# DeltaNet on one core: VectorE makes each slot's low weight tile behind the next slot's steps

## The chip, the core and the metric

The kernel runs on one core of one Trainium2 chip. The metric is the time of one execution on the device in microseconds (us). Engines are named TensorE (PE in the profile, its weight loads PEld), VectorE (DVE), ScalarE (ACT), GpSimd (POOL) and SyncE (SP, which issues most DMAs).

## What is computed

A trunk of two layers over 256 tokens with 2048 channels, all in float32. Layer 0 is a gated DeltaNet with 32 value heads and a feed-forward network; layer 1 is a sparse attention with another feed-forward network. The change touches only the DeltaNet of layer 0:

```python
proj = x @ w_in                                # q, k, v, z, two gates
qkv = silu(causal_depthwise_conv(qkv, conv_w)) # 4 taps
q, k = l2_normalize(q), l2_normalize(k)
o = chunk_gated_delta_rule(q, k, v, g, beta)   # a triangular solve per head and chunk, then a state
o = rms_norm(o, out_norm_g) * silu(z)
return o @ w_out
```

## The kernel before

**Products in three parts.** To keep float32 accuracy at the speed of fp32r, each weight piece is split: ScalarE copies the raw piece (128 x 1024) to W_HI, rounded (`split_hi`, line 1194), and VectorE subtracts, W_LO = raw - W_HI (`split_lo`, line 1627). TensorE then runs 12 matmuls per piece, W_HI with X_HI, W_LO with X_HI, W_HI with X_LO (`products`, lines 733 to 735). Both splits have four buffers (WS = 4), and so has the raw ring (RAWS = 4).

**The counts that tie them.** ScalarE makes the W_HI tile of piece h + 4 once TensorE is done with piece h (`w_used`); VectorE follows once it is there (`hi_ready`); TensorE starts a piece once its low tile is there (`lo_ready`, line 727); SyncE loads the next raw piece into a buffer when its low tile is done (`feed`, line 2210).

**Iterations and slots.** The DeltaNet runs in ten iterations, one for each of eight groups of four heads and two more to drain. Iterations 2 to 6 are one loop and have the same order; 0, 1, 7, 8 and 9 are written out. An iteration has 32 slots. A slot has at most one weight piece (parts qk, v, z of the input projection, out or old of the output projection), and behind it the steps of the delta rule that tables assign to it: SOLVE_STEPS for the group before, PREP_STEPS for the present one. Every engine walks the same 32 slots and does its own part of each step. In the loop, slots 0 to 7 hold qk, 8 to 15 v, and 16 to 31 z and out in pairs. Iterations 1, 7 and 8 have fewer pieces in the upper slots (PIECES_1, PIECES_7, PIECES_8).

**VectorE in a slot.** In `gdn_vector`: first the addition of an output stripe to H (`add_to_h`, line 1652, odd slots of out), then the steps (lines 1858 and 1859), then the low tile of the piece four further on. If the slot is in LO_HELD, this tile is kept back and made behind the next slot's steps (lines 1860 to 1862). Iterations 0 and 9 hold nothing. HI_HELD is the same for ScalarE and is empty.

**Steps that the text names, with VectorE's lines in the loop.** t0 to t3 (line 1802) and u0 to u5 (1808, 1810) in slots 1, 2, 4, 5, 7, 11, 15 and 16: rounds of the triangular inverse; nw (1815, 1816) in 16; ks (1822, 1825) in 21; kkqk (1769, 1774) in 25; osum (1834, 1835) in 26; oscale (1839, 1841) in 27, whose second part waits for GpSimd; init and masks (1780 to 1791) in 29; o_t (1661, tile A_LO or B_LO) in 31; dif (1757) in 7; the convolution taps (1686) in slots 2, 3, 5, 9, 11 and 12. In iterations 1, 7 and 8 the slots differ a little; ks is in 23, 21 and 15, and t2 of iteration 8 in 4.

Of the kernel before, what the change touches and what calls it, by code (L numbers as in the profile page):

```python
# [311 lines left out]


HI_HELD = ()
LO_HELD = (1, 2, 4, 6, 14)


def gdn_steps(it, hs):
# [206 lines left out]
def build(nc, stream, consts, params, tails, w2, gfin, x, xt, out):  # L525
# [18 lines left out]
    with ctx:  # L544
# [1077 lines left out]
        def split_lo(dve, c, h):  # L1622

            if isinstance(c, int) and c + h >= O_END:
                return
            dve.wait_ge(hi_ready, c + (h + 1))
            nc.vector.tensor_tensor(W_LO[:, h % WS, :], raw_piece(h), W_HI[:, h % WS, :].bitcast(f32),  # L1627
                                    SUB).then_inc(lo_ready, 1)
# [216 lines left out]
        def gdn_vector(dve, link, it):  # L1845
# [3 lines left out]
            for hs in range(32):  # L1849
# [10 lines left out]
                if held is not None:  # L1860
                    split_lo(dve, c, held)
                held = h + WS if part and hs in LO_HELD and not first and not last else None
                if part and held is None:
# [635 lines left out]
```

## Time and profile before

| | |
|---|---|
| time, median of 3 | 2801.64 us (2800.51 to 2804.14) |
| the profiled execution | 2803.94 us, span 2802.1 us |
| TensorE matmul busy | 2739.6 us, 98% |
| TensorE weight load busy | 2282.1 us, 81% |
| VectorE busy | 2219.6 us, 79% |
| ScalarE busy | 1648.4 us, 59% |
| mean granted TensorE clock | 0.995 |
| DMA | 493.23 MB, mean 176 GB/s |

The span is the time from the first to the last instruction of the profiled execution. TensorE's busy time is modelled for pipelined matmuls, so gaps between them say more than their sum. The DeltaNet takes the first third of the span, until about 955 us; one looped iteration takes 111.18 us.

### The profile page before, as it was taken

Reading aid. Unit: us, or ns where it says so; the run is one execution under the profiler, and the core shown is the slowest. Engines: PE = TensorE matmul, PEld = TensorE weight load, DVE = VectorE, ACT = ScalarE, POOL = GpSimd, SP = SyncE. Lnnn points to the kernel's source line nnn. Section 1 sums busy time; section 2 is a strip of 40 time slices with the busy share of each in tenths; the row PEclk is TensorE's granted clock in tenths of the full one; section 3 lists DMA queues with packets and bytes.
Section 4 is the critical chain, followed back from the end, with each engine's and each line's share of the span. In section 5 each row is a group of like instructions: output and inputs, shape, how many; then the busy total and the mean of one; then the engine's idle time right before and its main releaser. Section 6 shows DMA issues by size and latency. Waiting matters only on the chain.

```text
span 2802.1 us, 40252 instructions
## 1 busy us (share of the span) xinstructions
PE 2739.6 (98%) x13456; PEld 2282.1 (81%) x13456; DVE 2219.6 (79%) x2727; ACT 1648.4 (59%) x2184; POOL 31.0 (1%) x30
## 2 busy tenths in 40 slices
PE   8999999999988999999999999999999999999998
PEld 6878888888877888888888888888887888888887
DVE  5867877878767788888888876557677888888887
ACT  6766767667665555555555555554555555555554
POOL 0000000000000000000000000000000000000000
PEclk9999999999999999999999999999999999999999
DMA  6534444445433566656666656643345666656664
GB/s 239 181 124 153 159 144 163 156 149 167 158 105 113 166 210 199 198 185 203 198 198 203 198 172 224 222 135 114 106 158 188 207 199 200 199 184 200 198 201 166
DMA packets 135097, 493.23 MB, mean 176 GB/s; under 512 B 15009, under 2 KB 15329, under 8 KB 134625
## 3 DMA queue, kind: packets, MB, share of 16 engines
q1 hardware_dynamic: 133776, 487.82, 52.8%
q10 hardware_dynamic: 1232, 4.23, 0.4%
q8 instruction: 57, 0.93, 0.1%
q14 instruction: 32, 0.25, 0.0%
HBM read 489.86 MB, written 2.13 MB: 176 GB/s over the span
## 4 chain that ended last, share of the span: by engine, by line
PE 65%; issue 29%; DVE 3%; ACT 2%; DMA 1%; POOL 0%; POOLq 0%; DVEq 0%; SPq 0%; ACTq 0%
PE ACC L733 10%; PE ACC L735 10%; PE ACC L734 10%; PE SIDE L943 7%; PE SIDE L944 7%; PE SIDE L945 7%; PE ACC L943 3%; PE ACC L944 3%; PE ACC L945 3%; PE SIDE L741 2%; DVE W_LO L1627 1%; DMA RAW<-stream 1%; PE SIDE L1138 1%; ACT W_HI L1194 0%; ACT WORK L1587 0%
## 5 line engine op out<-in xcount | busy, mean ns | idle before, releaser
L1627 DVE TENSOR_TENSOR W_LO<-RAW,W_HI 128x1024 fp32r<-128x1024 f32 x424 | 511.6, 1222 | 268.9 <-ACT W_HI L1194 265.8
L1194 ACT ACTIVATE W_HI<-RAW 128x1024 fp32r<-128x1024 f32 x424 | 443.3, 1057 | 217.5 <-PE ACC L735 183.8
L1436 ACT ACTIVATE W_HI<-WORK 128x1024 fp32r<-128x1024 f32 x320 | 325.4, 1031 | 345.8 <-PE SIDE L945 232.7
L733 PE MATMUL ACC<-W_HI,X_HI 128*128 128x512 f32 x1216 | 491.2, 404 | 17.7 <-DVE W_LO L1627 17.6
L735 PE MATMUL ACC<-W_HI,X_LO 128*128 128x512 f32 x1216 | 477.6, 393 | 0.0
L734 PE MATMUL ACC<-W_LO,X_HI 128*128 128x512 f32 x1216 | 476.7, 392 | 0.0
L1878 DVE TENSOR_TENSOR W_LO<-WORK,W_HI 128x1024 fp32r<-128x1024 f32 x300 | 364.5, 1221 | 119.0 <-ACT W_HI L1436 116.3
L1436 ACT ACTIVATE W_HI<-RAW 128x1024 fp32r<-128x1024 f32 x328 | 314.8, 980 | 237.0 <-PE ACC L735 141.6
L733 PE MATMUL ACC<-W_HI,A_HI 128*128 128x512 f32 x928 | 370.3, 399 | 0.7 <-issue 0.7
L735 PE MATMUL ACC<-W_HI,A_LO 128*128 128x512 f32 x928 | 362.7, 391 | 0.0
L734 PE MATMUL ACC<-W_LO,A_HI 128*128 128x512 f32 x928 | 362.2, 390 | 0.0
L1878 DVE TENSOR_TENSOR W_LO<-RAW,W_HI 128x1024 fp32r<-128x1024 f32 x268 | 325.3, 1220 | 22.1 <-ACT W_HI L1436 17.3
L943 PE MATMUL SIDE<-W_HI,X_HI 128*128 128x512 f32 x800 | 311.4, 389 | 0.0
L945 PE MATMUL SIDE<-W_HI,X_LO 128*128 128x512 f32 x800 | 311.3, 389 | 0.0
L944 PE MATMUL SIDE<-W_LO,X_HI 128*128 128x512 f32 x800 | 311.3, 389 | 0.0
L733 PEld LDWEIGHTS ACC<-W_HI,X_HI 128*128 128x128 f32 x1216 | 230.0, 189 | 64.2 <-issue 15.6
L735 PEld LDWEIGHTS ACC<-W_HI,X_LO 128*128 128x128 f32 x1216 | 229.8, 189 | 50.4
L734 PEld LDWEIGHTS ACC<-W_LO,X_HI 128*128 128x128 f32 x1216 | 230.6, 190 | 43.6 <-issue 0.2
L735 PEld LDWEIGHTS ACC<-W_HI,A_LO 128*128 128x128 f32 x928 | 174.7, 188 | 37.2
L733 PEld LDWEIGHTS ACC<-W_HI,A_HI 128*128 128x128 f32 x928 | 174.9, 188 | 36.9 <-issue 2.3
L734 PEld LDWEIGHTS ACC<-W_LO,A_HI 128*128 128x128 f32 x928 | 174.9, 188 | 36.0 <-issue 1.2
L1652 DVE TENSOR_TENSOR H<-H,ACC 128x1024 f32<-128x1024 f32 x135 | 164.3, 1217 | 14.9 <-PE ACC L735 14.6
(363 smaller groups left out, 3798.7 us busy)
## 6 DMA issues: line engine op xcount, KB each, us to landing
RAW<-stream SPq DMA_DIRECT2D x752, 512.0 KB, 4.6
WORK<-stream SPq DMA_DIRECT2D x160, 512.0 KB, 4.8
WORK<-gdn_rows ACTq DMA_DIRECT2D x8, 512.0 KB, 6.2
WORK<-xt SPq DMA_DIRECT2D x4, 512.0 KB, 9.3
H<-x SPq DMA_DIRECT2D x2, 1024.0 KB, 13.6
out<-WORK SPq DMA_DIRECT2D x4, 512.0 KB, 3.5
WORK<-tails SPq DMA_DIRECT2D x2, 512.0 KB, 10.8
WORK<-gfin SPq DMA_DIRECT2D x1, 1024.0 KB, 6.6
```

The source lines that it names most:

```text
L733: nc.tensor.matmul(dst, hi[:, at:at + P], wh, start=first and h % 2 == 0 and q == 0, stop=False)
L734: nc.tensor.matmul(dst, hi[:, at:at + P], wl, start=False, stop=False)
L735: m = nc.tensor.matmul(dst, lo[:, at:at + P], wh, start=False, stop=last and h % 2 == 1 and q == 1)
L741: m = nc.tensor.transpose(SIDE[p][:, to:to + P], src, ident)
L943: nc.tensor.matmul(dst, hi, wh, start=start, stop=False)
L944: nc.tensor.matmul(dst, hi, wl, start=False, stop=False)
L945: return nc.tensor.matmul(dst, lo, wh, start=False, stop=stop)
L1194: nc.scalar.activation(W_HI[:, h % WS, :], raw_piece(h), ACT.Copy).then_inc(hi_ready, 1)
L1436: nc.scalar.activation(dst, src, ACT.Copy).then_inc(hi_ready, 1)
L1627: nc.vector.tensor_tensor(W_LO[:, h % WS, :], raw_piece(h), W_HI[:, h % WS, :].bitcast(f32), SUB).then_inc(lo_ready, 1)
L1652: nc.vector.tensor_tensor(dst, dst, tiles2(ACC[acc][:, :]), ADD).then_inc(acc_out[acc], 1)
L1878: nc.vector.tensor_tensor(lo, src, hi, SUB).then_inc(lo_ready, 1)
```

## The change

The tuple of slots whose low tile is held back goes from five slots to slots 0 to 30.

```diff
 HI_HELD = ()
-LO_HELD = (1, 2, 4, 6, 14)
+LO_HELD = tuple(range(31))
```

In iterations 1 to 8 VectorE then does, in every slot but 0 and 31, the addition to H and the steps, and behind them the low tile of the slot before. Slot 0 makes no tile, and slot 31 makes two if it has a piece of its own. Nothing else changes: the same instructions run on the same data, and the orders of the other engines stay.

## Rows read from the trace of the kernel before

**Rows 1.** The page: busy us (share of the span) xinstructions; DMA issues, us to landing.
```profile
PE 2739.6 (98%) x13456; PEld 2282.1 (81%) x13456; DVE 2219.6 (79%) x2727; ACT 1648.4 (59%) x2184; POOL 31.0 (1%) x30
...
RAW<-stream SPq DMA_DIRECT2D x752, 512.0 KB, 4.6
```

**Rows 2.** Timeline of TensorE: start us, us, instruction [idle before <-releaser].
```profile
155.55 1.08 PE L786 MATMUL SIDE<-UR,NR 128*128 128x128 f32 x8 [0.98 <-DVE NR L1816]
...
173.91 1.13 PE L786 MATMUL SIDE<-WORK 128*128 128x128 f32 x8 [2.54 <-DVE WORK L1825]
248.65 2.02 PE L786 MATMUL SIDE<-TR,WORK 128*128 128x128 f32 x16 [0.88 <-ACT TR L1350]
...
693.37 2.02 PE L786 MATMUL SIDE<-TR,WORK 128*128 128x128 f32 x16 [0.88 <-ACT TR L1350]
...
856.44 0.64 PE L793 MATMUL SIDE<-YQ,UQ 128*32 128x128 f32 x8 [1.89 <-issue]
873.75 0.63 PE L793 MATMUL SIDE<-YQ,UQ 128*32 128x128 f32 x8 [2.50 <-issue]
898.13 1.08 PE L786 MATMUL SIDE<-UR,NR 128*128 128x128 f32 x8 [0.84 <-DVE NR L1816]
```

**Rows 3.** Timeline of VectorE in iteration 3, slots 7 to 12 and 25 to 28.
```profile
333.79 3.49 DVE L1627 TENSOR_TENSOR W_LO<-RAW,W_HI 128x1024 fp32r<-128x1024 f32 x3
338.29 1.80 DVE L1686 SCALAR_TENSOR_TENSOR WORK<-WORK,CW 128x256 f32<-128x256 f32 x4 [1.01 <-ACT WORK L1284]
...
342.84 1.15 DVE L1802 TENSOR_TENSOR TR<-TR,SIDE 32x128 fp32r<-32x128 f32 x4
...
347.94 1.23 DVE L1627 TENSOR_TENSOR W_LO<-RAW,W_HI 128x1024 fp32r<-128x1024 f32 x1 [0.19 <-ACT W_HI L1194]
...
397.97 2.36 DVE L1769 TENSOR_TENSOR WORK<-SIDE,WORK 128x1024 f32<-128x1024 f32 x2 [1.05 <-PE SIDE L851]
...
401.78 1.21 DVE L1627 TENSOR_TENSOR W_LO<-RAW,W_HI 128x1024 fp32r<-128x1024 f32 x1
...
407.79 1.23 DVE L1841 TENSOR_TENSOR WORK<-WORK,SM 128x1024 f32<-128x1024 f32 x1
408.93 2.36 DVE L1627 TENSOR_TENSOR W_LO<-RAW,W_HI 128x1024 fp32r<-128x1024 f32 x2
```

**Rows 4.** A late tile (chain of waits), TensorE behind it; first matmuls of slots 14, 28, 30.
```profile
25.30 1.23 DVE W_LO L1627
...
26.67 0.47 PE L733 MATMUL ACC<-W_HI,X_HI 128*128 128x512 f32 x1 [1.33 <-DVE W_LO L1627]
...
348.05 0.48 PE L733 MATMUL ACC<-W_HI,X_HI 128*128 128x512 f32 x1
...
403.25 0.39 PE L733 MATMUL ACC<-W_HI,X_HI 128*128 128x512 f32 x1
...
408.96 0.39 PE L733 MATMUL ACC<-W_HI,A_HI 128*128 128x512 f32 x1
```

**Rows 5.** Timelines of three engines ahead of four gaps (864.77: the chain of waits).
```profile
149.11 1.22 DVE L1627 TENSOR_TENSOR W_LO<-RAW,W_HI 128x1024 fp32r<-128x1024 f32 x1 [4.44 <-ACT W_HI L1194]
...
149.10 0.59 ACT L1350 ACTIVATE TR<-SIDE 64x512 fp32r<-64x512 f32 x1
...
169.48 1.89 PE L901 MATMUL SIDE<-WORK,QK 128*128 128x256 f32 x8
...
170.90 1.23 DVE L1627 TENSOR_TENSOR W_LO<-RAW,W_HI 128x1024 fp32r<-128x1024 f32 x1
...
863.79 2.35 DVE L1627 TENSOR_TENSOR W_LO<-RAW,W_HI 128x1024 fp32r<-128x1024 f32 x2
...
864.77 0.48 PE SIDE L793 x8
...
894.76 0.63 ACT L1365 ACTIVATE UR<-WORK 64x512 fp32r<-64x512 f32 x1 [0.71 <-DVE WORK L1810]
```

**Rows 6.** One window: PE, PEld, DVE, ACT, POOL busy, granted clock, DMA share, GB/s.
```profile
161.60:165.00 3.40, 3.40 (x10) 2.62 (x9) 1.20 (x1) 2.64 (x4) 0.00 (x0) 0.51 0.00 0
```

## Prediction

> **What bounds the kernel now.** I read the page's busy times first: TensorE's matmuls fill 98% of the span and VectorE 79% [rows 1]. The busy share of matmuls says little alone, so the next view was the waits of TensorE, as its timeline lists them: in the whole DeltaNet stage (0 to about 955 us) there are some 30 gaps, and the five looped iterations (it 2 to 6) have exactly one each, 0.88 us long, always at the same place: five rows 111.18 us apart, of which the first and the last stand in [rows 2]. So the body of the stage is a TensorE stream without slack: whatever makes TensorE wait there is added to the time in full, five times. Iterations 1, 7 and 8 have larger gaps [rows 2]. VectorE's idle fifth lies unevenly. The third view was VectorE's timeline of one iteration, laid against the starts of TensorE's products: it tells how long before its product each W_LO tile is ready. That lead, not VectorE's total work, is what the change spends.
>
> **What the change does to the order.** No instruction is added or taken away; only VectorE's order in iterations 1 to 8 changes. A W_LO tile made in slot s is used four pieces later. Before, it was made at the end of slot s; after, behind VectorE's steps of slot s+1. Where slot s+1 has no VectorE step, or s was already in the old tuple, nothing moves. In the looped body that leaves 16 slots: 0, 3, 8, 10, 11, 15, 17, 18, 20, 21, 22, 24, 25, 26, 28, 30. Another way to see it: in front of each block of steps VectorE has now made one tile fewer. Four pieces of lead cover this nearly everywhere, so I only look for places where a block is long or where blocks follow each other without idle time. Going through all 16 gives two.
>
> **Slot 10's tile, used in slot 14.** Iteration 3 [rows 3]: the three tiles from 333.79 are those of slots 6, 7 and 8, then VectorE idles 1.01 us for the convolution input (338.29), makes the tiles of slots 9 and 10, and runs t3, u3 and six convolution taps from 342.84; the tile at 347.94 is slot 11's. After the change only slots 6 and 7 come ahead of 338.29, the idle time before it is wasted, and slots 8 and 9 come behind it. Slot 10's tile has to wait for t3, u3 and the taps. The earlier blocks are also shifted: u1 now has slot 3's tile ahead of it where there was idle time before, which I carry through as 0.18 us at 338.29. So: taps 338.47 to 340.27, 0.12 for the semaphore, two tiles at a pitch of 1.14, t3 at 342.68, and 5.02 us later (347.94 less 342.84, less the part of the wait that is ScalarE's) slot 10's tile, 347.70 to 348.92. TensorE restarts 0.14 us behind a late tile (26.67 less 26.53), so at 349.06, where it now starts at 348.05 [rows 4]. Stall: 1.0 us. Iterations 1 to 7 have these steps in nearly these slots (in 1 and 7 the same sum gives 1.0 too): 7 x 1.0 = **+7.0 us**. Bounds: 0, if VectorE reaches t3 one microsecond sooner; 1.3 if the 0.18 doubles and some latencies are longer, 9 in all.
>
> **Slot 26's tile, used in slot 30.** The tile at 401.78 and the first of the two at 408.93 are those of slots 25 and 27 [rows 3]; slot 26's lies between, behind osum. kkqk before them waits for TensorE (it starts at 397.97 whatever the order), and from there to 415 VectorE has no idle time but one wait. So the instants stay and the tiles move by one: slot 24's at 401.78, slot 25's behind osum, slot 26's at 408.93, behind add_to_h and both oscale steps (407.79). It is ready at 408.93 + 1.22 = 410.15, TensorE could start at 410.29, and today it starts at 408.96 [rows 4]: a stall of 1.33 us. This exists only in the body, since iterations 1, 7 and 8 have few pieces in slots 24 to 31: 5 x 1.33 = **+6.7 us**. Bounds: 1.0 and 1.5 each. Slot 24's tile, ready at 402.99, is in time for slot 28 (403.25 [rows 4], less 0.14) by about 0.1 us; slot 28's for slot 0 only because the stall has just moved TensorE; either could add 0.1 to 0.3 us.
>
> **Everything else of the move.** The other 14 slots keep their lead by the same walk, if only 0.1 us in slots 24 and 28, and cost nothing: TensorE's products cover them. VectorE also frees the RAW buffer later, and the SyncE queue issues the next load behind that count. A load lands 4.6 us after issue [rows 1] and ScalarE needs it one product (2.7 us) after the tile is used, so a tile ready less than about 2 us before its product makes ScalarE wait: 0.3 us for slots 10 and 24, behind which ScalarE has more idle time than that. Cost 0; if that cover were gone, 0.3 us more a time.
>
> **What it gives back.** A step that no longer stands behind a tile helps only where TensorE waits on it. In the body it never does: the 0.88 us is TensorE waiting for ScalarE's copy of t5 in the same slot [rows 2]. In iteration 1, u5 could start at 149.69 (ScalarE's TR) but stands behind the tile 149.11 to 150.33: 0.64 us of the 0.98 us gap at 155.55. ks could start at 171.37, and stands behind the tile of 170.90 to 172.13: 0.63 us of the gap at 173.91. In iteration 8, t2 is there at 865.25 but starts behind two tiles (to 866.14): about 0.7 us of the 2.50 us gap at 873.75; and ScalarE's idle 0.71 us at 894.76, behind u5, is freed, so 0.7 us of the gap at 898.13 [rows 2, 5]. Together **-2.7 us**. In its last slots iteration 8 loses about 0.9 us, as two tiles come ahead of osum, and gets it back at 928 where TensorE waits for A_LO today. Bounds of the gain: 0 (all given back behind it) and, with the clock, 7.8.
>
> **The clock.** TensorE fell to its lower level, 1.2 GHz, for 3.4 us six times in this stage, each time behind an idle gap of between 1.89 us (at 856.44) and 2.54 us (at 173.91) [rows 2]; one of them is 161.60 to 165.00, with a mean grant of 0.51 [rows 6]. Each costs half of 3.4, 1.7 us. Gaps of 0.88 [rows 2] and of 1.33 us at the start [rows 4] were not followed by one. My new stalls are 1.0 and 1.33 us, so I count none; two of the old six (behind 173.91 and 873.75) have their gaps shortened and may vanish: 0 to -3.4, taken as 0. The Trainium skill (TensorE: Matmul & The Clock Gate, section "Why this matters for your kernels") advises to keep idle gaps out of the matmul stream since TensorE otherwise goes back to half its clock. [...]
>
> **Sum.** 7.0 + 6.7 - 2.7 = +11.0 us. The profiled execution took 2803.94 us with a span of 2802.1; it would come to 2814.9. It lies 2.3 us above the median of 2801.64, to which the same 11.0 gives 2812.6 us, 0.39% slower. A measurement of this kernel can tell about 0.2%, 5.6 us, from no change.
>
> **Rivals.**
> - *Only one stall is real* (chance 0.18). The lead in slot 14 is sensitive: if t3 comes 1 us earlier, or the tiles pack closer, the first term is 0 and the time 2801.6 + 6.7 - 2.7 = 2805.6, within the bound. For it: only 1 us decides. Against it: the block t3, u3, taps is fixed at 5 us, and two tiles in front of it are a fixed 2.3.
> - *The stalls cost clock as well* (chance 0.17). If each of the five stalls before slot 30, or the tight slot 28 with it, is followed by 3.4 us at the lower level, 5 x 1.7 = 8.5 is added: 2821. For it: the clock does fall in this kernel after gaps not twice as long. Against it: the 1.33 us gap at 26.67 was not followed by a fall.
> - *Faster* (chance 0.05). The steps go first and the tiles are still in time. Mechanism: VectorE fills the time that it now idles before the tiles, and both late tiles arrive by their products; then only the gains are left, -2.7 and up to 3 x 1.7 of clock: 2798.9 down to 2793.8. It decides from the point where slot 26's tile is ready at 408.82 instead of 410.15, which would need one whole tile less between 397.97 and there [rows 3]. The rule of the Trainium skill (Trace Analysis, section "Optimization Strategy") is to find the gaps of the contended engine and let what it waits for start sooner. By it the change would be right, since steps do end most gaps; rows show that this holds for four of them only.
> - *My forecast* (chance 0.60): both stalls, 2812.6. Its own range is 2807 to 2818: below, the stalls without the 0.18 and the 0.14 (7 x 0.7 and 5 x 1.0), the gains, and one clock fall less; above, both stalls at their upper bounds (9 and 7.5) and nothing given back.
>
> **Range and chances.** Low end: the one-stall case with a clock fall less, 2804. High end: five falls more and the small terms of slots 28 and 0, 2823. Slower by over 0.2% (2807.2): forecast and clock rival, 0.77. Within: most of the one-stall case and the fringe, 0.18. Faster by over 0.2%: 0.05, the last rival's stronger end and what I overlooked.
>
> **What would show it.** In the profile after: one gap of about 1.3 us per looped iteration, released by W_LO of line 1627, in front of the product of slot 30; one of about 1.0 us in slot 14, in front of L733 behind the L807 block; an iteration period of 113.5 us instead of 111.18; the line "PE ACC L733 <- DVE W_LO L1627" of the waits up from 17.6 by some 13 us; gaps at 155.55, 173.91, 873.75 and 898.13 shorter by 0.6 to 0.7; all stages behind the DeltaNet stage the same length. I am wrong if the period stays at 111.2 (tiles in time), if the gaps are there but released by ScalarE or a DMA (the load path was the tighter one), or if the granted clock falls within the body.

## Result and profile after

The change makes the kernel slower, by about what was forecast.

| | before | after |
|---|---|---|
| time, median of 10 runs each | 2800.66 us (2797.92 to 2804.14) | 2808.66 us (2806.30 to 2810.79) |
| ratio after / before | | 1.0030, interval 1.0022 to 1.0038 |
| the profiled execution | 2803.94 us, span 2802.1 us | 2810.79 us, span 2809.0 us |
| mean granted TensorE clock | 0.995 | 0.997 |

The difference of the medians is 8.0 us, that of the profiled spans 6.9 us. The page of after has the same instruction counts, nearly the same busy times and the same load path [rows 1]:

```profile
PE 2738.9 (98%) x13456; PEld 2277.9 (81%) x13456; DVE 2216.9 (79%) x2727; ACT 1646.0 (59%) x2184; POOL 29.9 (1%) x30
```

What differs are TensorE's gaps. Its timeline after, first two of the looped iterations, then the four places where the change was to give something back:

```profile
348.78 0.50 PE L733 MATMUL ACC<-W_HI,X_HI 128*128 128x512 f32 x1 [0.58 <-DVE W_LO L1627]
...
410.96 0.50 PE L733 MATMUL ACC<-W_HI,A_HI 128*128 128x512 f32 x1 [1.04 <-DVE W_LO L1627]
...
524.29 0.50 PE L733 MATMUL ACC<-W_HI,A_HI 128*128 128x512 f32 x1 [1.04 <-DVE W_LO L1627]
```

```profile
155.46 1.08 PE L786 MATMUL SIDE<-UR,NR 128*128 128x128 f32 x8 [0.33 <-DVE NR L1816]
...
173.26 1.13 PE L786 MATMUL SIDE<-WORK 128*128 128x128 f32 x8 [1.98 <-DVE WORK L1825]
...
881.62 0.94 PE L793 MATMUL SIDE<-YQ,UQ 128*32 128x128 f32 x8 [1.94 <-issue]
...
905.34 1.08 PE L786 MATMUL SIDE<-UR,NR 128*128 128x128 f32 x8
...
931.95 1.07 PE L741 MATMUL SIDE<-K,WORK 128*128 128x128 f32 x8 [0.85 <-DVE WORK L1841]
```

Each looped iteration has two new gaps, both released by W_LO of line 1627: 0.58 us in front of the product of slot 14 and 1.02 to 1.04 us in front of that of slot 30. From 410.96 to 524.29 an iteration takes 113.33 us, where it took 111.18 [rows 2]: 2.15 us more, five times. Against [rows 2] the gap at 155.55 went from 0.98 to 0.33, that at 173.91 from 2.54 to 1.98, that at 873.75 from 2.50 to 1.94, and that at 898.13 (here at 905.34) is gone. The last row is a new gap at the end of iteration 8, where two tiles now come ahead of osum. Not every gap shrank: one of 0.72 us stands at 873.02, where the first profile of the kernel before has none; its second profile, at the end of the experiments, has it too, so it does not belong to the change.

The waits of TensorE, their first line before and after, say the same in one number: 13 such waits more, 9.2 us of idle time more (the prediction had said some 13 us; the last section tells why the idle time comes out lower than the delay).

```profile
PE ACC L733 <- DVE W_LO L1627: 17.6, 8, 11.0
```

```profile
PE ACC L733 <- DVE W_LO L1627: 26.8, 21, 10.9
```

VectorE's timeline of iteration 3 after, beside [rows 3]:

```profile
333.98 2.36 DVE L1627 TENSOR_TENSOR W_LO<-RAW,W_HI 128x1024 fp32r<-128x1024 f32 x2
338.27 1.80 DVE L1686 SCALAR_TENSOR_TENSOR WORK<-WORK,CW 128x256 f32<-128x256 f32 x4 [1.94 <-ACT WORK L1284]
340.20 2.36 DVE L1627 TENSOR_TENSOR W_LO<-RAW,W_HI 128x1024 fp32r<-128x1024 f32 x2
342.48 1.15 DVE L1802 TENSOR_TENSOR TR<-TR,SIDE 32x128 fp32r<-32x128 f32 x4
343.66 1.25 DVE L1808 STREAM_TRANSPOSE WORK<-TR 128x1024 f32<-128x1024 f32 x1
344.83 2.55 DVE L1686 SCALAR_TENSOR_TENSOR WORK<-WORK,CW 128x256 f32<-128x256 f32 x6
347.50 1.23 DVE L1627 TENSOR_TENSOR W_LO<-RAW,W_HI 128x1024 fp32r<-128x1024 f32 x1
...
405.01 1.23 DVE L1627 TENSOR_TENSOR W_LO<-RAW,W_HI 128x1024 fp32r<-128x1024 f32 x1
406.16 1.22 DVE L1652 TENSOR_TENSOR H<-H,ACC 128x1024 f32<-128x1024 f32 x1
407.29 1.22 DVE L1839 TENSOR_TENSOR WORK<-WORK 128x1024 f32<-128x1024 f32 x1
408.54 1.22 DVE L1841 TENSOR_TENSOR WORK<-WORK,SM 128x1024 f32<-128x1024 f32 x1
409.68 2.35 DVE L1627 TENSOR_TENSOR W_LO<-RAW,W_HI 128x1024 fp32r<-128x1024 f32 x2
```

The wait for the convolution input grew from 1.01 to 1.94 us (one tile fewer ahead of it), two tiles stand behind the taps, and slot 10's tile at 347.50, behind t3, u3 and the six taps, ends at 348.73; TensorE starts slot 14 at 348.78. Slot 26's tile is the first of the two at 409.68, behind both oscale steps; it ends at 410.90 and TensorE starts slot 30 at 410.96. Those are the two chains of the forecast.

### The profile page after: what moved, and what is told of

It is laid out like the page before. It is cut to its first block, busy times and chain, and to the rows that moved or that the text cites. A ratio compares the mean times of both kernels' runs of the same rounds, so it can differ in the third digit from the quotient of the medians.

```text
span 2809.0 us, 40247 instructions
## 1 busy us (share of the span) xinstructions
PE 2738.9 (98%) x13456; PEld 2277.9 (81%) x13456; DVE 2216.9 (79%) x2727; ACT 1646.0 (59%) x2184; POOL 29.9 (1%) x30
## 4 chain that ended last, share of the span: by engine, by line
PE 62%; issue 32%; DVE 2%; ACT 2%; DMA 2%; POOL 0%; POOLq 0%; DVEq 0%; SPq 0%; ACTq 0%
PE ACC L733 10%; PE ACC L735 10%; PE ACC L734 9%; PE SIDE L945 7%; PE SIDE L943 7%; PE SIDE L944 7%; PE ACC L943 3%; PE ACC L945 3%; PE ACC L944 3%; PE SIDE L741 2%; DMA RAW<-stream 1%; DVE W_LO L1627 1%; PE SIDE L1138 1%; ACT W_HI L1194 0%; ACT WORK L1587 0%
```

## Experiments

Every kernel changes only which slots are in LO_HELD. Ratios are to runs of the kernel before in the same session, whose medians were 2799.2, 2799.9 and 2800.0 us. The last column is the time from one looped iteration to the next.

| kept back | time, us | ratio (interval) | looped iteration, us |
|---|---|---|---|
| all but 26 | 2821.47 | 1.0081 (1.0068 to 1.0095) | 115.97 |
| all but 10 | 2802.22 | 1.0012 (1.0002 to 1.0021) | 112.6 |
| all but 10 and 26 | 2813.58 | 1.0051 (1.0037 to 1.0065) | 115.2, once 113.6 |
| all, in the loop only | 2811.65 | 1.0042 (1.0029 to 1.0056) | 113.3 |
| all, outside the loop only | 2798.60 | 0.9996 (0.9987 to 1.0005) | 111.18 |
| old five, 3, 11, 15, 22 | 2797.17 | 0.9990 (0.9981 to 0.9999) | 111.18 |
| old five and 26 | 2800.95 | 1.0004 (0.9995 to 1.0013) | 111.41 |
| all but 24 | 2805.11 | 1.0019 (1.0009 to 1.0028) | 112.70 |
| all but 26 and 28 | 2802.05 | 1.0008 (0.9999 to 1.0017) | 111.9 to 112.0 |
| all but 10 and 24 | 2799.78 | 0.9999 (0.9990 to 1.0008) | 111.9 |

**Each stall undone alone.**

```diff
-LO_HELD = tuple(range(31))
+LO_HELD = tuple(n for n in range(31) if n != 10)
```

> The changed kernel, but slot 10's tile is made in its own slot. Theory (late tiles): the idle 0.58 us (0.79 us of delay) in front of slot 14 goes in the five looped iterations and 0.42 us (about 0.6) in iterations 1 and 7: 5 x 0.79 + 2 x 0.6 = 5.2 us, period 113.33 -> 112.5 us, time 2803.5 us. Rival (t3, u3 and the taps are as urgent as the tile): they start 1.1 us later, ScalarE copies u3 later and y4 waits in slot 13, so that the period changes by less than 0.2 us and the time stays at 2808.

The gaps in slot 14 were gone and those in slot 30 stayed at 1.02 to 1.07 us. The iteration took 112.6 us (from 359.65 to 472.25), so slot 30 alone costs 1.4 us an iteration. That part of the theory is shown. The time was 2802.22 us, near the 2803.5 expected.

```diff
-LO_HELD = tuple(range(31))
+LO_HELD = tuple(n for n in range(31) if n != 26)
```

> The changed kernel, but slot 26's tile is made in its own slot. Theory (late tiles): this tile alone makes the stall before slot 30, 1.04 us of idle and 1.36 us of delay in each looped iteration of the changed kernel. It is now ready about 1.5 us before its product; period 113.33 -> 112.0 us, time 2808.7 - 5 x 1.36 = 2801.9 us. Rival (VectorE's idle time before kkqk is what is lost, and comes back elsewhere): oscale moves 1.14 us back, and ScalarE's z stripe, the masks and the next iteration's y0 with it; the stall moves to slot 0 or 31 and the period stays above 113 us, time 2807 to 2809.

The slowest kernel of the study: 2821.47 us. The stall in slot 30 was gone, but a larger one stood in front of slot 0 of the next iteration, five times, and the clock fell behind each. TensorE's timeline at the third of them, VectorE's ahead of the second (at 422.74), and the window behind the second (granted clock in the last column but two):

```profile
538.71 0.50 PE L733 MATMUL ACC<-W_HI,X_HI 128*128 128x512 f32 x1 [2.12 <-DVE W_LO L1627]
```

```profile
403.12 2.35 DVE L1769 TENSOR_TENSOR WORK<-SIDE,WORK 128x1024 f32<-128x1024 f32 x2 [2.52 <-PE SIDE L851]
...
414.07 1.23 DVE L1841 TENSOR_TENSOR WORK<-WORK,SM 128x1024 f32<-128x1024 f32 x1
...
419.54 0.42 DVE L1785 TENSOR_TENSOR WORK<-NQ,K 128x256 f32<-128x256 f32 x1 [2.42 <-ACT NQ L1317]
...
420.34 1.22 DVE L1791 TENSOR_TENSOR YB<-NQ,K 128x1024 fp32r<-128x1024 f32 x1
421.47 2.35 DVE L1627 TENSOR_TENSOR W_LO<-RAW,W_HI 128x1024 fp32r<-128x1024 f32 x2
```

```profile
423.56:426.97 3.41, 3.41 (x10) 2.63 (x8) 3.41 (x4) 0.96 (x2) 0.00 (x0) 0.50 0.80 243
```

The tile at 421.47 is slot 28's. It stands behind the masks (1785 to 1791), and these waited 2.42 us for ScalarE's NQ. ScalarE had stood idle before that, waiting for the second oscale step:

```profile
415.38 1.28 ACT L1204 ACT_TABLE_LOAD   x1 [1.71 <-DVE WORK L1841]
```

So a tile more ahead of oscale (slot 26's, 1.14 us) came back through ScalarE to the tile of slot 28. VectorE in the same places of the kernel of the change:

```profile
398.73 2.36 DVE L1769 TENSOR_TENSOR WORK<-SIDE,WORK 128x1024 f32<-128x1024 f32 x2 [2.52 <-PE SIDE L851]
...
414.00 0.42 DVE L1785 TENSOR_TENSOR WORK<-NQ,K 128x256 f32<-128x256 f32 x1 [1.29 <-ACT NQ L1317]
...
415.94 2.36 DVE L1627 TENSOR_TENSOR W_LO<-RAW,W_HI 128x1024 fp32r<-128x1024 f32 x2
```

There slot 28's tile is ready at 417.16, and TensorE starts slot 0 at 417.34: in time by 0.18 us, and only because the stall of slot 30 has delayed TensorE, as the prediction said of it. Counted from kkqk (line 1769), whose start TensorE sets, the tile begins 17.21 us later in this kernel (398.73 to 415.94) and 18.35 us later with slot 26 taken out (403.12 to 421.47). The difference is 1.14 us, one tile: the way through GpSimd and ScalarE added nothing to it. The size of the new stall follows: 1.14 us for the tile, and about 1.36 us because TensorE no longer loses time at slot 30, less the 0.18 us in hand, make 2.3 us of delay behind an idle row of 2.12 us. With 0.8 us for slot 14 and 1.7 us for the clock, 111.18 comes to 116.0 us, and 115.97 was measured.

**Both stalls undone.** The same edit with both 10 and 26 taken out.

> Both slots 10 and 26 at once. Theory: both stalls go and add up: the period is that of before, 111.2 us, and what is left is what the change gives back in iterations 1 and 8 and in the clock: 2808.7 - 6.8 - 5.2 = 2796.7 us, 4 us or 0.14% faster than before. Rival (the stalls hide each other, one fewer makes the other longer): 2800 us or more, period over 111.6 us.

2813.58 us, where 2796.7 was expected: the gaps in slot 14 were gone, but in front of slot 0 stood gaps of 2.10 to 2.22 us, as in the kernel without 26. With the two late tiles of the forecast repaired, the change is still 0.5% slower than before. The stalls of slots 30 and 0 are not independent terms: the one appears when the other is taken out.

**Slot 28's tile.** To test that it is this tile's place, and not a backlog of VectorE as a whole:

```diff
-LO_HELD = tuple(range(31))
+LO_HELD = tuple(n for n in range(31) if n not in (26, 28))
```

> All slots are kept back but 26 and 28. Theory: in the kernel without 26 the late tile is slot 28's, because it stands behind init and the masks of slot 29, and these wait for ScalarE. Made in its own slot it stands ahead of them, so the gap of 2.12 us in front of slot 0 is gone, the clock no longer falls there, only the stall in slot 14 is left (0.79 us), and the looped iteration takes 111.18 + 0.79 = 112.0 us instead of 115.97: 2821.5 - 5 x 4.0 = 2801.6 us. Rival: VectorE as a whole is behind in slots 26 to 29 because of one more tile ahead of oscale, and the order in slot 29 matters little: a gap of 0.5 to 1.1 us stays in front of slot 0 and the iteration takes 112.5 to 113.1 us, 2804 to 2807 us in all.

No gap was left in front of slot 0, the clock did not fall in the loop, and the iteration took 111.9 to 112.0 us, 2802.05 us in all, as the theory had it (112.0 and 2801.6). VectorE's timeline in iteration 3:

```profile
409.49 2.35 DVE L1627 TENSOR_TENSOR W_LO<-RAW,W_HI 128x1024 fp32r<-128x1024 f32 x2
...
413.81 0.43 DVE L1785 TENSOR_TENSOR WORK<-NQ,K 128x256 f32<-128x256 f32 x1 [1.30 <-ACT NQ L1317]
```

The two tiles at 409.49 are those of slots 27 and 28, so slot 28's is done before the wait for NQ. The 0.57 us gap in slot 14 was all that was left, and it is worth 0.73 to 0.83 us an iteration (111.91 to 112.01 less 111.18).

**One tile less ahead of oscale.** Slot 24's tile back in its own slot, ahead of the wait for kkqk:

```diff
-LO_HELD = tuple(range(31))
+LO_HELD = tuple(n for n in range(31) if n != 24)
```

> The changed kernel, but slot 24's tile is made in its own slot, in VectorE's idle time before kkqk. Theory: from kkqk to slot 26's tile VectorE has no slack, so one tile less there brings that tile 1.14 us forward: the stall before slot 30 falls from 1.36 to about 0.2 us: period 112.2 us, time 2808.7 - 5.7 = 2803.0 us. Rival (it waits for GpSimd's power in oscale, not for VectorE's work): less than 0.3 us an iteration is won, 2807 us or more.

The stall in slot 30 was gone but for some 0.25 us: slot 26's tile ran from 407.92 to 409.14, and TensorE started slot 30 at 409.20, just behind it. A small gap stood as well, 0.17 to 0.27 us in front of slot 0, behind slot 28's tile. In its timeline:

```profile
416.00 0.50 PE L733 MATMUL ACC<-W_HI,X_HI 128*128 128x512 f32 x1 [0.17 <-DVE W_LO L1627]
```

Slot 28's tile is the first of two that VectorE makes from 414.73, so it is done at 415.95. The iteration took 112.70 us, 0.63 us less than with the change, and the time was 2805.11 us, 2 us more than expected: of the 1.4 us that slot 30 had cost, about 0.25 stayed there and 0.45 came back in front of slot 0. The same with 10 taken out too:

> All slots are kept back but 10 and 24. Theory: without 24 the stall before slot 30 was gone and 0.17 to 0.27 us stood in front of slot 0; without 10 as well the stall in slot 14 goes too, 5 x 0.79 in the loop and 2 x 0.6 in iterations 1 and 7, so the looped iteration takes 112.70 - 0.79 = 111.9 us and the time is 2805.1 - 5.1 = 2800 us, the same as the kernel before within 0.1%. Rival: as when 10 alone was undone, what is taken from slot 14 is partly given back later, here in front of slot 0, where the tile does not move with TensorE: the gap there grows to about 1 us, the iteration stays at 112.6, and the time at 2804.

2799.78 us, with no gap in slot 14, 0.16 to 0.29 us in front of slot 0, and an iteration of 111.9 us (from 359.37 to 471.26): the theory's numbers. Its ratio is 0.9999: 14 of the 16 slots moved in the loop cost 0.7 us an iteration together, and the gains outside the loop pay for that.

**Slot 26 alone kept back.** The old five and 26.

```diff
-LO_HELD = tuple(range(31))
+LO_HELD = (1, 2, 4, 6, 14, 26)
```

> The kernel before, with only slot 26 added to the held ones. Theory: the tile waits for add_to_h and oscale, but one tile fewer stands before it than in the changed kernel, so it is late by about 0.5 us instead of 1.3: 5 x 0.5 = +2.5 us, 2803.2 us, with a W_LO gap in front of slot 30. Rival (being behind oscale is the whole cause, how many tiles stand before it does not matter): 5 x 1.36 = +6.8, 2807.5 us.

2800.95 us, and no stall of the full size: the iteration took 111.41 us, 0.23 us more, half of the 0.5 expected. VectorE's timeline says why:

```profile
396.71 2.36 DVE L1769 TENSOR_TENSOR WORK<-SIDE,WORK 128x1024 f32<-128x1024 f32 x2 [1.04 <-PE SIDE L851]
...
400.52 1.21 DVE L1627 TENSOR_TENSOR W_LO<-RAW,W_HI 128x1024 fp32r<-128x1024 f32 x1
...
405.36 1.23 DVE L1841 TENSOR_TENSOR WORK<-WORK,SM 128x1024 f32<-128x1024 f32 x1
406.50 3.49 DVE L1627 TENSOR_TENSOR W_LO<-RAW,W_HI 128x1024 fp32r<-128x1024 f32 x3
```

Behind kkqk, whose start TensorE sets, stands one tile (slot 25's, at 400.52) ahead of slot 26's at 406.50; with the whole change there are two, slots 24's and 25's. One tile less is 1.14 us, and the stall of 1.33 to 1.42 us less 1.14 is 0.19 to 0.28, with 0.23 us measured. So the stall of slot 30 is not slot 26's alone: it needs slot 24's tile moved behind the wait for kkqk as well. Undoing either takes away most of it or all, as the kernels without 24 and without 26 showed.

**Loop and ends apart.** The change in iterations 2 to 6 alone, and in 1, 7 and 8 alone.

```diff
+LO_OLD = (1, 2, 4, 6, 14)
...
-                held = h + WS if part and hs in LO_HELD and not first and not last else None
+                held = h + WS if part and hs in (LO_OLD if isinstance(it, int) else LO_HELD) and not first and not last else None
```

> Steps first in every slot of the looped iterations 2 to 6 only; iterations 1, 7 and 8 keep the old order. Theory: all of the loss and none of the gain: the period is 113.3 us, 5 x 2.15 = 10.75 us more than before: 2811.4 us, 0.38% slower, and the clock still falls six times. Rival (part of the loss lies outside the loop): less than 8 us slower than before.

> Steps first in iterations 1, 7 and 8 only; the loop keeps the old order. Theory: two stalls of 0.6 us in slot 14 of iterations 1 and 7, gains of 2.7 us in iterations 1 and 8, and two falls of the clock fewer (1.7 us each): 2800.7 + 1.2 - 2.7 - 3.4 = 2795.8 us; period 111.18 us. If the clock falls as often as before, 2799.2. Rival (nothing is given back, the clock is chance): 2800 to 2802 us.

The diff is that of the first; the kernel with the change outside the loop has LO_HELD and LO_OLD the other way round. In the loop alone the change costs 12.4 us (2811.65 against 2799.21), with both gaps and 113.3 us an iteration, as in the full change; 5 x 2.15 is 10.8, and the rest is within the interval of the ratio, 8 to 16 us. Its profile had three falls of the clock and not the six expected. Outside the loop alone it gives 1.3 us (2798.60 against 2799.93), which the interval does not tell from no difference; 2795.8 had been expected, or 2799.2 if the clock fell as often. Its gaps at 155.46 (0.33 us) and 173.25 (1.98 us) were as short as with the full change, and the gaps of slot 14 in iterations 1 and 7 were 0.4 us.

**Only the four slots that give.** The old five, and 3, 11, 15 and 22.

```diff
-LO_HELD = tuple(range(31))
+LO_HELD = (1, 2, 3, 4, 6, 11, 14, 15, 22)
```

> The kernel before, with slots 3, 11, 15 and 22 added to the held ones: the four tiles behind which a step stood that TensorE waited for (t2 and u5 of iteration 8, u5 and ks of iteration 1). Theory: the gaps at 155.55, 173.91, 873.75 and 898.13 shrink by 0.6 to 0.7 us each, 2.7 us in all, and no stall appears: 2798.0 us, or down to 2794.6 if two falls of the clock go too; period 111.18 us. Rival (the gain comes only with all slots held): 2800.7 us, no change.

2797.17 us, 0.10% under the kernel before (interval 0.01% to 0.19%), and the lowest median of all kernels here. With ten kernels compared, an interval that only just leaves out 1 is weak evidence of a gain; the shorter gaps are plain. The loop was untouched (111.18 us), and the gaps had the short values:

```profile
154.75 0.52 PE L786 MATMUL SIDE<-UR,NR 128*128 128x128 f32 x3 [0.33 <-DVE NR L1816]
...
171.19 0.46 PE L786 MATMUL SIDE<-WORK 128*128 128x128 f32 x2 [1.98 <-DVE WORK L1825]
...
869.68 0.52 PE L793 MATMUL SIDE<-YQ,UQ 128*32 128x128 f32 x6 [1.94 <-issue]
```

**The kernel before, profiled again.** Nothing is changed; the question is the clock.

> The kernel before, once more, for its falls of the clock alone. The profiled execution had six of them in the DeltaNet stage, the kernels that differ from it by a few slots had three. Theory: the number changes from one execution to the next with the same order of work, so another profile of the same kernel shows three to five, and a span lower by 1.7 us for each one less than six. Rival: the number belongs to the order; then six again at 161.6, 175.2, 813.5, 827.2, 857.9 and 875.0, and a span of 2802 us.

It had two falls in the DeltaNet stage (at about 173 and 839 us), fewer even than the three to five expected, a time of 2797.33 us and a span of 2795.5 us, 6.6 us below the first profile's 2802.1. The same windows in the two executions of the same kernel, first the earlier one:

```profile
812.00:832.00 20.00, 14.79 (x73) 13.09 (x74) 8.95 (x13) 8.73 (x11) 0.00 (x0) 0.83 0.22 72
856.00:878.00 22.00, 19.05 (x99) 15.38 (x100) 19.10 (x32) 12.71 (x24) 0.00 (x0) 0.85 0.43 142
```

```profile
812.00:832.00 20.00, 14.76 (x85) 12.18 (x86) 11.36 (x16) 11.51 (x17) 1.88 (x1) 1.00 0.18 58
856.00:878.00 22.00, 17.90 (x106) 14.20 (x104) 17.98 (x27) 14.99 (x25) 0.00 (x0) 1.00 0.40 127
```

It is tempting to divide 6.6 us by the four falls that are missing, but the traces say otherwise. One instant near the end of the stage (line 741) and one far behind it, first in the earlier execution and then in the later, with a gap of the later one that comes up below:

```profile
953.50 1.06 PE L741 MATMUL SIDE<-K,H 128*128 128x128 f32 x8 [0.53 <-DVE H L1652]
...
2130.45 0.50 PE L733 MATMUL ACC<-W_HI,X_HI 128*128 128x512 f32 x1 [2.45 <-DVE W_LO L1627]
```

```profile
871.10 0.64 PE L793 MATMUL SIDE<-YQ,UQ 128*32 128x128 f32 x8 [3.21 <-issue]
...
950.71 1.06 PE L741 MATMUL SIDE<-K,H 128*128 128x128 f32 x8 [0.53 <-DVE H L1652]
...
2125.52 0.50 PE L733 MATMUL ACC<-W_HI,X_HI 128*128 128x512 f32 x1 [0.40 <-DVE W_LO L1627]
```

At the end of the stage the two are only 2.8 us apart, 0.7 us for each fall. A fall costs little where TensorE soon waits for another engine anyway: from the start at 847.92 to that at 873.75 [rows 2] the earlier execution took 25.8 us with a fall inside, and the later one took 25.7 without (845.42 to 871.10), because its gaps there are 1.73, 0.73 and 3.21 us instead of 1.89 and 2.50 us. The other 3.8 us lie at 2130 us, where the earlier execution waited 2.05 us longer, behind a tile whose raw piece landed later (VectorE waited 6.29 us for that load, and 4.22 us in the later execution), and then had a seventh fall. So neither the number of falls nor that wait belongs to the order of work alone; both change between executions of one kernel.

## Why the prediction was right

The direction, the mechanism and both places were right; the sum of +11.0 us was 3 us too large against the measured 8.0 (interval 6.2 to 10.6). The terms:

- **Slot 10's tile, +7.0.** The mechanism is shown (the tile ends at 348.73, the gap goes when slot 10 is undone); the size was too large. The kernel without 26 and 28 isolates it: about 0.8 us an iteration, so 5 x 0.8, and about 0.6 in each of iterations 1 and 7 (gaps of about 0.4 us there, and the 0.2 us by which the delay exceeds the gap in the loop): 5.2 us. Two small steps were off. The 0.18 us carried through to 338.29 was not there: the taps began at 338.27, since ScalarE's input sets that instant. And TensorE restarted 0.05 us behind the tile (348.78 less 348.73), not 0.14. Without the two, 1.0 comes to 0.74 us.
- **Slot 26's tile, +6.7.** 1.33 us was forecast; 1.33 to 1.42 were measured (113.33 less 111.91 to 112.01, and 112.6 less 111.18 from the kernel without 10) an iteration, some 6.8 us. The prediction's reason was complete here: all tiles behind kkqk move by one, slot 24's among them.
- **What it gives back, -2.7.** Iteration 1 gave 0.65 and 0.56 us. (For ks the rows give 172.13 less 171.37, 0.76 us, where the prediction wrote 0.63; for t2 866.14 less 865.25, 0.89, where it wrote about 0.7.) In iteration 8 the gaps also depend on where the clock fell, so two profiles with the same fall there (one, at about 839 us) are laid side by side: outside the loop alone, and the second one of the kernel before. The gap that the first profile shows as 2.50 us is 1.95 against 3.21, the one of 0.84 is gone, and 0.2 us are lost at the end of the iteration, where a gap of 0.85 us stands in place of one of 0.72: 1.9 us. Together 3.1 us.
- **The clock, 0.** In the profiled executions it fell four times in the stage against six, and over the whole span four times against seven (the last few microseconds of each left out). The prediction had two fewer as a possibility of the change. The second profile of the kernel before shows two in the stage with nothing changed, so the difference between two single profiles says nothing of the order. The price of 1.7 us a fall is near the 1.6 us measured in the loop (last section), but too high for this stage as a whole: the five falls of the first profile that the second has not are worth 0.2 to 1.4 us each where they stand in the stage. Whether the change makes falls rarer on average was not measured.

Together 5.2 + 6.8 - 3.1 = 8.9 us, beside 8.0 us for the medians, well inside the interval. The difference of the profiled spans, 6.9 us, cannot be used so: it holds two falls fewer in the stage, and a third fewer at 2130 us, where the gap of 2.45 us of the kernel before is 2.64 us after. That it comes near the 8.0 is luck.

Of the rivals, one stall alone and faster are out by the rows above. The clock rival did not happen in the change, but its price was real where the gaps were longer: the kernel without slot 26 had five falls at the places where its 2.1 us gaps stood, and came to 2821.47 us. What the prediction did not see is how near this was. It said that slot 28's tile is in time only because of the stall at slot 30, and that held: the changed kernel loses nothing there. It did not work out that case further: once the stall is repaired by making slot 26's tile ahead of oscale, 2.1 us of gap and up to 1.7 us of clock take its place. The step that lacked is to follow a tile that is put in front of a step through the other engines back to VectorE, with TensorE's products at their places without the stall.

## What to carry to other kernels

Where one in-order engine makes tiles for a bound engine and also does steps in between, go by the lead of each tile at its consumer, slot by slot, and move only those whose lead is spare and whose step ends a wait: here four slots gave something, two late tiles cost 10.8 us in the loop, and keeping back the four beside the old five gave the lowest median. A stall that is taken out moves the bound engine forward on every later tile, so before repairing one, look at the lead of the next tiles: repairing slot 26 alone took the kernel from 8 to 22 us above the kernel before. A difference of a few microseconds between two single profiles can be the clock or one late load, so compare the period of an iteration and the gaps, and not the spans.

## What the runs showed of the hardware

**The same gap does not always cost clock.** In the kernel without 10 and 26, the idle time in front of slot 0 is 2.10 us at 419.27 and at 534.47. Behind the first the clock fell, behind the second it did not:

```profile
419.20:425.20 6.00, 5.93 (x25) 4.65 (x26) 5.74 (x6) 2.62 (x5) 0.00 (x0) 0.72 0.57 177
534.40:540.40 6.00, 5.93 (x32) 4.90 (x33) 5.74 (x6) 4.18 (x7) 0.00 (x0) 1.00 0.62 194
```

Three of its five gaps were followed by a fall; the iterations took 115.2 us with one and 113.6 without, 1.6 us for 3.4 us at half clock. Gaps of up to 1.07 us in the loop were followed by none in any kernel. The length of the gap does not decide alone: the 3.21 us gap at 871.10 above was not followed by a fall (the clock was 1.00 in the window from 856 to 878), nor the 2.64 us gap at 2138.93 of the changed kernel, while the one of 1.89 us at 856.44 [rows 2] was. The Trainium skill (TensorE: Matmul & The Clock Gate, section "Why this matters for your kernels") advises against long idle gaps in the matmul stream, since TensorE otherwise goes back to half its clock. These traces agree that gaps can cost the clock, but the falls here came behind gaps shorter than those that the page warns of.

**A stall costs more than its idle row.** A gap of 0.57 us lengthened the iteration by 0.73 to 0.83 us, and one of 1.04 us by 1.4 us. The starts in the changed kernel, at the stall of slot 30, show most of the difference:

```profile
409.52 0.39 PE L735 MATMUL ACC<-W_HI,X_LO 128*128 128x512 f32 x1
410.96 0.50 PE L733 MATMUL ACC<-W_HI,A_HI 128*128 128x512 f32 x1 [1.04 <-DVE W_LO L1627]
411.29 0.39 PE L734 MATMUL ACC<-W_LO,A_HI 128*128 128x512 f32 x1
411.52 0.40 PE L735 MATMUL ACC<-W_HI,A_LO 128*128 128x512 f32 x1
```

In the stream a matmul starts 0.23 us behind the one before it, though each is printed 0.39 us long: they overlap by 0.16 us. The idle time is counted from the printed end, so it leaves this out: 410.96 less 409.52 is 1.44 us, 1.21 more than 0.23. The first matmul behind the stall then takes 0.33 us to the next start, 0.10 more. Together 1.31 us; less than 0.1 us is left open. So a stall is better read from the starts than from the idle time.
